# Up projections of a two-level fast product: where the first half's weight sums stand, which bank the last product uses, and who makes two of those sums

## The chip, the cores and the metric

The kernel runs on one core of one Trainium2 chip. The metric is device time in microseconds (us) of one launch. TensorE multiplies, VectorE (DVE in the rows) adds and subtracts, ScalarE (ACT) copies and applies activations, GpSimd (POOL) issues the accumulating transfers and copies small edges, SyncE (SP) issues the plain loads.

## The reference, cut to what matters

One inference step of a two-layer decoder trunk in float32, for 512 prompt rows and 32 sample rows. Each layer has a token mixer and a convolutional feed-forward part, and this is the part that the change touches:

```
u = h @ w_up                      # 544 x 1024 times 1024 x 8192
c = conv_b + sum(conv_w[j] * full[:, j:j + T] for j in range(3))
y = gelu(c[..., :4096]) * c[..., 4096:]
out = y @ w_down
```

## The kernel before

The up projection of a layer is cut into 32 groups g. A group is 128 columns of the gelu side ("a") and 128 of the gate side ("g"), over all 544 tokens, and is computed as a 2 x 2 block product with seven block products in place of eight (the Winograd form of Strassen's scheme): sums of weight blocks and sums of token blocks are multiplied, and DVE joins the products afterwards. Tokens are split in halves of 272.

From group 4 on, two groups make a "set" s (`DEEP`, 14 sets in a layer, groups 2s and 2s+1). In a set, product 1 and product 2 of both groups are themselves split: for z = 0 (gate-side weights) and z = 1 (sums of the a side), seven small products of 136 tokens (`deep_products`, in the order 1, 2, 6, 7, 5, 3, 4) take their weights from blocks of the ring and from four weight sums s3, s1, s2, s4 in `DS[z]`, and their tokens from `HT` and from four token sums in `DT`. DVE makes the weight sums (`deep_sums(s, z)`) one set ahead, ACT copies the first small product (`deep_copy`), and DVE joins the seven (`deep_joins`).

Then `deep_group` runs the remaining five products of each group, in the order 4, 1, 3, 5, 6, each into one PSUM bank (`deep_bank`). Product 6 shares the bank of product 1, so TensorE holds it until DVE has read product 1:

```
return 4 * (g % 2) + {4: 2, 1: 1, 3: 0, 5: 3, 6: 1}[j]
...
pe.wait_ge(s_ev, EV0[l] + 7 * u + 2)
product(deep_bank(g, 6), s4, b22, True, True).then_inc(s_pr, 1)
```

`s_ev` counts DVE's seven joins of a group in the order u2 (reads product 4), three of u3 (the first reads product 1), c11 (product 3), c21 (product 5), c12 (product 6).

Weights come in 1 MB loads into a ring of four slots, two slots a set. SP issues both loads of set s+1 when set s-1's products have ended, so at the start of set s: first the a side, then the g side. POOL issues two kinds of accumulating transfers: `first_sums`, which adds one half of the a-side slot to the other (512 KB, semaphore `s_sig1`; z = 1's sums of set s+1 and later weight sums wait for it), and `third_sums`, which adds a block of `w_up` to a base that SP has loaded (256 KB each, `s_base3` and `s_sig3`). POOL's queue also holds the small copies of the convolution's edges.

DVE's order in a set is written by hand in its `deep(s)`:

```
deep_part(s, g0, ("u2",))
deep_sums(s + 1, 0)
deep_part(s, g0, ("u3", "c11", "c21", "c12"))
deep_sums(s + 1, 1)
deep_part(s, g1, ("u2",))
deep_weights(g0 + 2, ("s2", "s4"))
```

and it goes on with the convolution and gate of group 2s, u3 and c11 of group 2s+1, another weight sum, and c21 of 2s+1; c12 of 2s+1 is the first work of the next set. `deep_sums(s + 1, 0)` waits for the g-side load, `deep_sums(s + 1, 1)` for `s_sig1`. ACT's order in a set begins with the convolution's first tap of group 2s-1, a side (`newest`, waits for that group's c21), then the copy of z = 0's first small product; TensorE's small product 3 of z = 0, which goes into the same bank as the copied one, waits for that copy.

Of the kernel before, what the change touches and what calls it, by code (L numbers as in the profile page):

```python
# [14 lines left out]
ALU = mybir.AluOpType  # L15
# [225 lines left out]
def trunk(nc, A, O, at, n_const):  # L241
    ctx = ExitStack()
    with ctx:
# [305 lines left out]
        s_cst2, s_tkm, s_md1, s_sne, s_sna, s_cp, s_cpe, s_qx, s_tkv, s_row = s_kce, s_kc, s_t1, s_gl, s_t2, s_bp, s_bpe, s_at, s_ate, s_imp  # L549
        s_lp, s_ls, s_lc, s_lt, s_xl = (sem(n) for n in ("s_lp", "s_ls", "s_lc", "s_lt", "s_xl"))  # L550
        s_base3 = s_wbk
        s_sig1, s_sig3 = ([sem(f"{n}{b}") for b in range(2)] for n in ("s_sig1", "s_sig3"))
        s_sop, s_soe, s_soo = (sem(n) for n in ("s_sop", "s_soe", "s_soo"))
        s_fp, s_fo = sem("s_fp"), sem("s_fo")
# [2044 lines left out]

        def deep_bank(g, j):  # L2600

            return 4 * (g % 2) + {4: 2, 1: 1, 3: 0, 5: 3, 6: 1}[j]

        def deep_copied(l, s, z):

# [34 lines left out]
        def _(sp):  # L2640
# [54 lines left out]
            def ffn_loads(l):  # L2695

                sp.wait_ge(s_mm, (M_AO0 + 3, M_MO0 + 1)[l])
                if l == 0:
                    sp.wait_ge(s_kvo, 16 * (1 + 2 * NB))
                rows = A["state_ffn_conv"][l].rearrange("b r (t c q) -> c (b r) t q", c=8, q=P)  # L2700
                for c in range(8):
                    sp.dma_start(SI[16 * c:16 * c + 16], rows[c]).then_inc(s_sil, 16)

                def third_bases(g0):
                    for g in (g0, g0 + 1):
                        c = sum_columns(g) + FF
                        sp.wait_ge(s_pr, deep_done(l, g - 2, 1))
                        sp.dma_start(WS[g % 2][:, 1], w_up[l][:, 0:4, c:c + P]).then_inc(s_base3[g % 2], 16)

                for k in range(32):  # L2710
                    k0 = W_UP[l] + k
                    i, j = divmod(k, 4)
                    if i == 0:
                        sp.wait_ge(s_mm, (M_AO, M_MO)[l] + 2 * (j + 1))
                    else:
                        sp.wait_ge(s_pr, PR0[l] + 7 * (FU * l + 4 * (i - 1) + (2, 2, 4, 4)[j]))
                    col = i * 512 + (j // 2) * 256 + (j % 2) * FF
                    sp.dma_start(R[:, k0 % RING], w_up[l][:, :, col:col + 256]).then_inc(s_w[k0 % RING], 16)
                    if i and j % 2:
                        third_bases(2 * (k // 2))  # L2720
                    if l == 0 and k == 3:
                        sp.wait_ge(s_nrm, normed(1, 1) + 8)
                        sp.dma_start(hsc[:, :], XTF[:, :]).then_inc(s_xl, 16)
                for d in range(FD):
                    if d < 3:
                        sp.wait_ge(s_pr, PR0[l] + 7 * (FU * l + (30, 30, 32)[d]))
                    else:
                        sp.wait_ge(s_mm, M_DN[l] + d - 2)
                    sp.dma_start(R[:, DN_RING[d % 3]], w_dn[l][d % 4, :, :, (d // 4) * 256:(d // 4 + 1) * 256])\
                        .then_inc(s_dw[d % 3], 16)  # L2730
                    if l == 0 and d == 4:
                        sp.wait_ge(s_xl, 16)
                        sp.dma_start(XTF[:, :], hsc[:, :]).then_inc(s_xl, 16)
# [18 lines left out]
        def _(pe):  # L2752
# [336 lines left out]
            def ffn(l):  # L3089
# [62 lines left out]
                def deep_group(s, g):  # L3152

                    u, z, e = FU * l + g, g % 2, deep_set(l, s, g % 2)
                    a11, a12, a21, a22 = up_blocks(l, g)
                    s2, s3, s4 = (WS[g % 2][:, q] for q in range(3))
                    su = SU0[l] + 4 * (u + FD * l)
                    pe.wait_ge(s_su, su + 3)
                    pe.wait_ge(s_lc, 4 * e + 3)
                    product(deep_bank(g, 4), s2, t2, True, True).then_inc(s_pr, 1 if z else 5)  # L3160
                    pe.wait_ge(s_sig3[g % 2], third_sum(l, g))
                    product(deep_bank(g, 1), s3, t3, True, True).then_inc(s_pr, 1)
                    product(deep_bank(g, 3), a12, b21, True, True).then_inc(s_pr, 1)
                    pe.wait_ge(s_lc, 4 * e + 4)
                    product(deep_bank(g, 5), a22, t4, True, True).then_inc(s_pr, 1)
                    pe.wait_ge(s_su, su + 4)
                    pe.wait_ge(s_ev, EV0[l] + 7 * u + 2)
                    product(deep_bank(g, 6), s4, b22, True, True).then_inc(s_pr, 1)

                def deep(s):  # L3170
# [6 lines left out]
                        pe.wait_ge(s_ev, EV0[l] + 7 * u)  # L3177
                    else:
                        pe.wait_ge(s_ev, EV0[l] + 7 * (u - 1))
                    pe.wait_ge(s_lt, 4 * (l + 1))  # L3180
                    deep_products(s, 0)
                    pe.wait_ge(s_sig1[s % 2], first_sum(l, 2 * s))
                    pe.wait_ge(s_ev, EV0[l] + 7 * u)
# [56 lines left out]
                def bank_free(cp, j):  # L3240
                    u = FU * (l + 1)
                    if cp == 0:
                        pe.wait_ge(s_ev, EV0[l] + 7 * (u - 2) + (5, 7, 1, 6, 12, 14, 8)[j])
                    elif cp == 1 and j == 0:
                        pe.wait_ge(s_ev, EV0[l] + 7 * u)
                    else:
                        c, q = divmod(7 * cp + j - 8, 7)
                        c += 4 * l
                        if q in (0, 3, 4):
                            pe.wait_ge(s_da, 3 * c + (1, 0, 0, 2, 3)[q])  # L3250
                        else:
                            pe.wait_ge(s_de, 7 * c + (0, 1, 6, 0, 0, 2, 7)[q])
# [422 lines left out]
        def _(dve):  # L3675
# [444 lines left out]
            def ffn(l):  # L4120
# [68 lines left out]
                def deep_tokens():  # L4189
# [4 lines left out]
                        dve.wait_ge(s_xl, 16)  # L4194
                    dve.wait_ge(s_xs, XB0[l] + 5 * l + 2)
                    x = HT[:, 0:4, :].rearrange("p k (z q t) -> p k z q t", z=2, q=2)
                    x11, x12, x21, x22 = (x[:, k:k + 2, :, q, :] for k in (0, 2) for q in range(2))
                    t1, t2, t3, t4 = (DT[:, n] for n in range(4))
                    tt(t1, x12, x11, sub).then_inc(s_lt, 1)
                    tt(t3, x22, x12, sub).then_inc(s_lt, 1)  # L4200
                    dve.wait_ge(s_lt, 4 * l + 1)
                    tt(t2, x22, t1, sub).then_inc(s_lt, 1)
                    dve.wait_ge(s_lt, 4 * l + 3)
                    tt(t4, x21, t2, sub).then_inc(s_lt, 1)

                def deep_sums(s, z):
# [9 lines left out]
                        dve.wait_ge(s_sig1[s % 2], first_sum(l, 2 * s))  # L4216
                    if e >= 2:
                        dve.wait_ge(s_lp, 7 * (e - 2) + 7)
                    tt(s3, w11, w21, sub).then_inc(s_ls, 1)
                    tt(s1, w21, w22, add).then_inc(s_ls, 1)  # L4220
                    dve.wait_ge(s_ls, 4 * e + 2)
                    tt(s2, s1, w11, sub).then_inc(s_ls, 1)
                    dve.wait_ge(s_ls, 4 * e + 3)
                    tt(s4, w12, s2, sub).then_inc(s_ls, 1)

                def deep_weights(g, names):

# [23 lines left out]
                def deep_joins(s, z):  # L4251
# [13 lines left out]
                    tt(both.rearrange("p (a b t) -> p a b t", a=2, b=2)[:, :, 1, :], pair(DU[z]),  # L4265
                       PS[:, 4 * z:4 * z + 3:2, 0:q], add).then_inc(s_lc, 1)
                    dve.wait_ge(s_lp, 7 * e + 7)
                    tt(both[:, 2 * q:3 * q], DU[z][:, q:2 * q], PS[:, 4 * z + 3, 0:q], add).then_inc(s_lc, 1)

                def deep_part(s, g, names):  # L4270

# [2 lines left out]
                    p1, q7, q5 = P1T[g % 2], Q7T[g % 2], Q5T[g % 2]  # L4274
                    ua, ug = U[:, 2 * (g % 2), :], U[:, 2 * (g % 2) + 1, :]
                    ps = lambda j: PS[:, deep_bank(g, j), 0:HALF]
                    for name in names:
                        if name == "c11":
                            dve.wait_ge(s_pr, deep_done(l, g, 3))
                            dve.wait_ge(s_ul, 2 * (u - 1))  # L4280
                            tt(ug[:, 2:2 + HALF], p1, ps(3), add).then_inc(s_ev, 1)
                        elif name == "u2":
                            dve.wait_ge(s_lc, 4 * deep_set(l, s, 1) + 4)
                            dve.wait_ge(s_pr, deep_done(l, g, 4))
                            tt(DU[g % 2], p1, ps(4), sub).then_inc(s_ev, 1)
                        elif name == "u3":
                            dve.wait_ge(s_ev, ev + 1)
                            dve.wait_ge(s_pr, deep_done(l, g, 1))
                            tt(q7, DU[g % 2], ps(1), add).then_inc(s_ev, 1)  # L4289
                            tt(DU[g % 2], DU[g % 2], q5, sub).then_inc(s_ev, 1)  # L4290
                            dve.wait_ge(s_ev, ev + 2)
                            second_half(ua, q5, q7, sub).then_inc(s_ev, 1)
                        elif name == "c21":
# [2 lines left out]
                        else:  # L4296
                            dve.wait_ge(s_ev, ev + 3)
                            dve.wait_ge(s_pr, deep_done(l, g, 6))
                            second_half(ug, DU[g % 2], ps(6)).then_inc(s_ev, 1)

                def deep(s):

# [8 lines left out]
                    convolved(g0 - 1)  # L4311
                    deep_joins(s, 1)
                    gated(g0 - 1)
                    deep_part(s, g0, ("u2",))
                    deep_sums(s + 1, 0)
                    deep_part(s, g0, ("u3", "c11", "c21", "c12"))
                    deep_sums(s + 1, 1)
                    deep_part(s, g1, ("u2",))
                    deep_weights(g0 + 2, ("s2", "s4"))
# [138 lines left out]
        def _(pool):  # L4458
# [41 lines left out]
            def ffn(l):  # L4500
# [10 lines left out]
                def first_sums(g):  # L4511
# [2 lines left out]
                    pool.dma_start(R[:, ka % RING, 0:4, :], R[:, ka % RING, 4:8, :], accum_op=ALU.add)\  # L4514
                        .then_inc(s_sig1[g // 2 % 2], 16)

                def third_sums(g):
                    pool.wait_ge(s_base3[g % 2], 64 + third_sum(l, g))
                    c = sum_columns(g)
# [3 lines left out]
                for g in range(FU):  # L4523
                    k = FU * l + g
                    if g + 1 in BY_DMA:
                        third_sums(g + 1)
                    if g + 2 in BY_DMA and g % 2 == 0:
                        first_sums(g + 2)
                    for ag in range(2):
                        n = g + 32 * ag  # L4530
# [52 lines left out]
```

## Time and profile before

| what | us |
|---|---|
| median of 3 runs (lowest, highest) | 2100.52 (2100.24, 2101.18) |
| the profiled execution's own time | 2101.75 |
| span of its trace | 2100.0 |
| TensorE busy | 2051.7 (98%) |
| VectorE busy | 1429.6 (68%) |

The trace covers the span, and the profiled execution's own time is 1.75 us more. Sums below are made against that execution, which is 1.2 us above the median of the runs.

### The profile page before, as it was taken

To read this page: it belongs to the slowest core of one execution; us is meant where nothing else is said; L and a number is where in the kernel's file an instruction comes from. 1 tells how busy PE (TensorE), PEld (TensorE's weight loads), DVE (VectorE), ACT (ScalarE), POOL (GpSimd) and SP (SyncE) were. 2 spreads that over 40 slices of the span, in tenths; PEclk is the share of its full clock that TensorE was granted. 3 is DMA by queue.
4 is the path that set the end of the run, shared out by engine and by line. 5 is a ranking of instruction groups with operands and counts; after the bars stand their busy time and mean duration, and the time that the engine had idled before them with its cause. 6 is when DMAs were issued, how large, how long until landed. Compare 5 with 4: busy or idle time off the path is not lost.

```text
span 2100.0 us, 32975 instructions
## 1 busy us (share of the span) xinstructions
PE 2051.7 (98%) x11958; PEld 1647.9 (78%) x11958; DVE 1429.6 (68%) x3462; ACT 590.0 (28%) x1362; POOL 273.6 (13%) x583
## 2 busy tenths in 40 slices
PE   8999999998899999999999999999999999999998
PEld 7556777787788888888888775778888888888887
DVE  5257996677887888888323684655888888885223
ACT  3016886563321211221001220542311222210002
POOL 1002000000022222220000100410222222210001
PEclk9999999999999999999999999999999999999999
DMA  9128206994356666662321324253366666632223
GB/s 222 56 65 261 65 2 156 277 252 93 123 126 141 141 141 149 142 141 88 130 89 63 134 81 102 71 157 92 108 141 141 143 149 158 155 95 81 81 81 117
DMA packets 270962, 262.81 MB, mean 125 GB/s; under 512 B 42802, under 2 KB 251930, under 8 KB 270034
## 3 DMA queue, kind: packets, MB, share of 16 engines
q1 hardware_dynamic: 233186, 213.58, 35.3%
q0 software_dynamic: 37616, 47.12, 11.8%
q8 instruction: 97, 1.59, 0.3%
q14 instruction: 63, 0.52, 0.1%
HBM read 230.14 MB, written 24.16 MB: 121 GB/s over the span
## 4 chain that ended last, share of the span: by engine, by line
PE 88%; DVE 4%; DMA 3%; ACT 1%; SPq 1%; issue 1%; DVEq 0%; ACTq 0%
PE PS L3107 47%; PE PS L3149 7%; PE PS L1889 3%; PE PS L863 2%; PE PS L2906 2%; PE PS L1681 2%; PE PS L2885 2%; DMA ring<-in_w_ffn_up 2%; PE PS L1760 2%; PE PS L791 2%; PE PS L778 2%; PE PS L811 2%; PE PS L1633 2%; PE PS L3046 1%; PE PS L2915 1%
## 5 line engine op out<-in xcount | busy, mean ns | idle before, releaser
L3107 PE MATMUL PS<-arena,ring 128*128 128x272 f32 x1392 | 341.6, 392 | 0.0
L3107 PEld LDWEIGHTS PS<-arena,ring 128*128 128x128 f32 x1392 | 264.3, 190 | 54.5
L3570 ACT ACTIVATE arena<-arena,CB,CW 128x560 f32<-128x560 f32 x128 | 108.5, 853 | 392.2 <-DVE arena L4295 326.1
L4172 DVE SCALAR_TENSOR_TENSOR arena<-arena,CW 128x560 f32<-128x560 f32 x256 | 187.9, 796 | 0.8 <-ACT arena L3570 0.8
L3107 PE MATMUL PS<-arena,CONST 128*128 128x272 f32 x768 | 187.1, 392 | 0.0
L3107 PE MATMUL PS<-arena 128*128 128x272 f32 x768 | 186.8, 392 | 0.0
L3107 PEld LDWEIGHTS PS<-arena,CONST 128*128 128x128 f32 x768 | 145.9, 190 | 30.1
L3107 PEld LDWEIGHTS PS<-arena 128*128 128x128 f32 x768 | 143.8, 190 | 27.8
L3107 PE MATMUL PS<-HT,ring 128*128 128x272 f32 x640 | 158.9, 393 | 2.3 <-DVE HT L4097 2.3
L3107 PEld LDWEIGHTS PS<-HT,ring 128*128 128x128 f32 x640 | 121.2, 190 | 28.1 <-ACT arena L3502 1.8
L4539 POOL COPY arena<-arena 128x16 f32<-128x16 f32 x128 | 42.1, 329 | 506.9 <-DVE arena L4295 404.2
L3107 PE MATMUL PS<-HT,arena 128*128 128x272 f32 x384 | 96.5, 394 | 4.1 <-DVE RR L4289 2.9
L3107 PE MATMUL PS<-HT,CONST 128*128 128x272 f32 x384 | 97.9, 398 | 2.1 <-DVE RR L4289 2.1
L3575 ACT ACTIVATE arena<-arena 128x560 f32<-128x560 f32 x64 | 43.0, 672 | 180.1 <-DVE arena L4172 180.1
L3107 PEld LDWEIGHTS PS<-HT,arena 128*128 128x128 f32 x384 | 71.9, 190 | 22.1 <-issue 7.8
L3107 PEld LDWEIGHTS PS<-HT,CONST 128*128 128x128 f32 x384 | 70.6, 190 | 23.4 <-issue 10.5
L3149 PE MATMUL PS<-XT 128*128 128x136 f32 x672 | 87.0, 279 | 0.0
L4082 DVE TENSOR_TENSOR arena<-ring 128x512 f32<-128x512 f32 x18 | 12.4, 690 | 109.0 <-PE PS L3107 109.0
L3149 PEld LDWEIGHTS PS<-XT 128*128 128x128 f32 x672 | 82.0, 190 | 0.0
L3636 ACT COPY RT<-PS 128x272 f32<-128x272 f32 x15 | 5.8, 386 | 270.8 <-PE PS L3107 270.8
L1121 ACT ACTIVATE arena<-arena 128x128 f32<-128x128 f32 (+3 forms) x128 | 70.7, 560 | 4.6 <-DVE arena L1275 4.6
L863 PE MATMUL PS<-arena 128*128 128x256 f32 x256 | 67.0, 386 | 2.1 <-DVE arena L1344 1.8
(609 smaller groups left out, 3827.5 us busy)
## 6 DMA issues: line engine op xcount, KB each, us to landing
ring<-in_w_ffn_up SPq DMA_DIRECT2D x64, 1024.0 KB, 6.4
ring<-in_w_ffn_down SPq DMA_DIRECT2D x32, 1024.0 KB, 5.2
ring<-in_cache_nsa_kv SPq DMA_DIRECT2D x128, 128.0 KB, 5.5
arena<-in_cache_nsa_kv SPq DMA_DIRECT2D x56, 256.0 KB, 6.7
ring<-ring POOLq DMA_DIRECT2D x28, 512.0 KB, 7.4
ring<-in_w_ml_in SPq DMA_DIRECT2D x12, 1024.0 KB, 6.8
arena<-in_cache_nsa_win SPq DMA_DIRECT2D x16, 512.0 KB, 6.7
out_nsa_win_sample<-in_cache_nsa_win POOLq DMA_DIRECT2D x8, 1016.0 KB, 17.9
```

What stands on the lines that cost most here:

```text
L778: last = mm(PS[:, 2 * (p % 2) + g2, c0:c0 + w], QT[rows, n, i * P:(i + 1) * P], KTS[rows, br - 1, n // 4, 0:w], start=True, stop=True)
L791: last = tr(PS[:, 4 + g2, k * P:(k + 1) * P], PB[:, u % 6, k * P:(k + 1) * P], ident)
L811: last = mm(out(g2, i), KVP[:, k, c0:c0 + 64], PTS[:, (2 * p + g2) % 4, s0 + k * P:s0 + (k + 1) * P], start=(p % NU == 0 and m == 0), stop ...
L863: last = mm(PS[:, 2 + c, 0:256], W1[:, c, a_, :], CT[:, (16 * n + 8 * b + a_) % 3, :, c, :], start=(a_ == 0), stop=(a_ == 7))
L1121: last = nc.scalar.activation(PB[:, u % 6, cols], SB[:, u % 4, cols], ACT.Exp, scale=-1.0, bias=ST[:, p % 4, 0, m, g2:g2 + 1], accum_out=S ...
L1889: last = mm(PS[:, bank, 0:HALF], R[:, r, k, (m % 2) * P:(m % 2 + 1) * P], turned_heads(k)[:, half(h)], start=(k == 0), stop=(k == KT - 1))
L3107: last = mm(PS[:, bank, 0:HALF], lhs[:, k, :], rhs(k), start=(first and k == 0), stop=(done and k == 3))
L3149: last = mm(PS[:, 4 * z + bank, half_], lhs[:, k, :], rhs[:, k, :], start=(k == 0), stop=(k == 1))
L3570: nc.scalar.activation(CV[:, 2 * (g % 2) + ag, :], U[:, 2 * (g % 2) + ag, 2:562], ACT.Identity, bias=cb[:, l, n:n + 1], scale=cw[:, l, 2, ...
L3575: nc.scalar.activation(CV[:, 2 * (g % 2), :], CV[:, 2 * (g % 2), :], ACT.Gelu_apprx_tanh)\
L4172: v.scalar_tensor_tensor(out=c, in0=U[:, 2 * (g % 2) + ag, tap:tap + 560], scalar=cw[:, l, tap, n:n + 1], in1=c, op0=ALU.mult, op1=ALU.add)\
L4539: g_.tensor_copy(ULS[:, n, :].rearrange("p (b r) -> p b r", b=NB), u[:, 514:562].rearrange("p (b s) -> p b s", b=NB)[:, :, 4:6])
```

## The change

- `deep_bank` puts product 6 into product 4's bank, and TensorE's wait ahead of product 6 is for one join of its group (u2) where it was for two. The waits of the down projection's first products for free banks (`bank_free`) are renumbered to match.
- In DVE's `deep(s)`, u3 of group 2s stands ahead of `deep_sums(s + 1, 0)`.
- For z = 0, s1 and s3 become plain sums of two blocks, w21 + w22 and w11 + w21. From set 3 on (13 sets a layer) DVE doesn't make them: SP loads two bases of 128 KB each into `DS[0]` (`deep_bases`, after the two ring loads), and POOL issues one accumulating transfer of 256 KB on top (`deep_accumulated`), ahead of `first_sums`. DVE waits for its semaphore `s_dsa` in `deep_sums(s + 1, 0)` and makes only s2 and s4.
- Signs follow: the token sums for z = 0 differ from those for z = 1, so `deep_tokens` has nine half-sized instructions for four, and some joins add where they subtracted.

```
-            return 4 * (g % 2) + {4: 2, 1: 1, 3: 0, 5: 3, 6: 1}[j]
+            return 4 * (g % 2) + {4: 2, 1: 1, 3: 0, 5: 3, 6: 2}[j]
+        def deep_got(l, s):
+            return 16 * (s - DEEP[0] + l * (len(DEEP) - 1))
...
+                def deep_bases(s):
+                    e = deep_set(l, s, 0)
+                    if e >= 2:
+                        sp.wait_ge(s_lp, 7 * (e - 2) + 7)
+                    c = sum_columns(2 * s) + FF
+                    for n in range(2):
+                        sp.dma_start(DS[0][:, n], w_up[l][:, 0:2, c + P * n:c + P * n + P]).then_inc(s_dsb, 16)
...
                     if i and j % 2:
+                        if k // 2 > DEEP[0]:
+                            deep_bases(k // 2)
                         third_bases(2 * (k // 2))
...
-                    pe.wait_ge(s_ev, EV0[l] + 7 * u + 2)
+                    pe.wait_ge(s_ev, EV0[l] + 7 * u + 1)
                     product(deep_bank(g, 6), s4, b22, True, True).then_inc(s_pr, 1)
...
-                        pe.wait_ge(s_ev, EV0[l] + 7 * (u - 2) + (5, 7, 1, 6, 12, 14, 8)[j])
+                        pe.wait_ge(s_ev, EV0[l] + 7 * (u - 2) + (5, 2, 7, 6, 12, 9, 14)[j])
...
-                    tt(s3, w11, w21, sub).then_inc(s_ls, 1)
-                    tt(s1, w21, w22, add).then_inc(s_ls, 1)
-                    dve.wait_ge(s_ls, 4 * e + 2)
-                    tt(s2, s1, w11, sub).then_inc(s_ls, 1)
+                    if z == 0 and s > DEEP[0]:
+                        dve.wait_ge(s_dsa, deep_got(l, s))
+                        dve.sem_inc(s_ls, 2)
+                    else:
+                        tt(s3, w11, w21, sub if z else add).then_inc(s_ls, 1)
+                        tt(s1, w21, w22, add).then_inc(s_ls, 1)
+                        dve.wait_ge(s_ls, 4 * e + 2)
+                    tt(s2, s1, w11, sub if z else add).then_inc(s_ls, 1)
                     dve.wait_ge(s_ls, 4 * e + 3)
-                    tt(s4, w12, s2, sub).then_inc(s_ls, 1)
+                    tt(s4, w12, s2, sub if z else add).then_inc(s_ls, 1)
...
-                    deep_part(s, g0, ("u2",))
+                    deep_part(s, g0, ("u2", "u3"))
                     deep_sums(s + 1, 0)
-                    deep_part(s, g0, ("u3", "c11", "c21", "c12"))
+                    deep_part(s, g0, ("c11", "c21", "c12"))
                     deep_sums(s + 1, 1)
...
+                def deep_accumulated(s):
+                    pool.wait_ge(s_dsb, 64 + 2 * deep_got(l, s))
+                    c = sum_columns(2 * s) + FF + P
+                    pool.dma_start(DS[0][:, 0:2].rearrange("p s k c -> p (s k) c"), w_up[l][:, 0:4, c:c + P], accum_op=ALU.add)\
+                        .then_inc(s_dsa, 16)
...
                     if g + 1 in BY_DMA:
                         third_sums(g + 1)
                     if g + 2 in BY_DMA and g % 2 == 0:
+                        if g // 2 + 1 > DEEP[0]:
+                            deep_accumulated(g // 2 + 1)
                         first_sums(g + 2)
```

## Rows read from the trace of the kernel before

**Rows 1.** The page, busy time of each engine, its share, instructions.

```profile
PE 2051.7 (98%) x11958; PEld 1647.9 (78%) x11958; DVE 1429.6 (68%) x3462; ACT 590.0 (28%) x1362; POOL 273.6 (13%) x583
```

**Rows 2.** TensorE's waits by releaser: total us, times, longest.

```profile
PE PS L3107 <- DVE RR L4289: 5.0, 6, 1.3
```

**Rows 3.** Busy time of one set, 869.15 to 894.10 us; PEclk, DMA share, GB/s last.

```profile
869.15:894.10 24.95, 24.95 (x138) 21.61 (x137) 20.98 (x51) 5.09 (x8) 6.41 (x15) 1.00 0.63 148
```

**Rows 4.** Timeline of TensorE in that set and the next one's start.

```profile
880.94 2.00 PE L3107 MATMUL PS<-arena,ring 128*128 128x272 f32 x8
882.78 2.00 PE L3107 MATMUL PS<-HT,arena 128*128 128x272 f32 x8
...
890.11 2.00 PE L3107 MATMUL PS<-arena,ring 128*128 128x272 f32 x8
892.00 2.07 PE L3107 MATMUL PS<-HT,CONST 128*128 128x272 f32 x8
...
896.22 0.63 PE L3149 MATMUL PS<-HT,XT 128*128 128x136 f32 x4
```

**Rows 5.** Timeline of SyncE's queue, the same stretch: issue time, length, line.

```profile
869.15 0.99 SPq L2718 DMA_DIRECT2D ring<-in_w_ffn_up  x2
...
894.10 0.99 SPq L2718 DMA_DIRECT2D ring<-in_w_ffn_up  x2
```

**Rows 6.** Timeline of DVE in the same set.

```profile
880.23 0.42 DVE L4219 TENSOR_TENSOR XT<-ring 128x256 f32<-128x256 f32 x1 [2.13 <-DMA ring<-in_w_ffn_up]
...
885.30 0.42 DVE L4219 TENSOR_TENSOR XT<-ring 128x256 f32<-128x256 f32 x1
...
886.90 0.42 DVE L4285 TENSOR_TENSOR arena<-RT,PS 128x272 f32<-128x272 f32 x1
...
894.19 0.44 DVE L4295 TENSOR_TENSOR arena<-PS,RR 128x272 f32<-128x272 f32 x1
```

**Rows 7.** Timeline of ACT at the next set's start.

```profile
894.67 0.86 ACT L3570 ACTIVATE arena<-arena,CB,CW 128x560 f32<-128x560 f32 x1 [3.17 <-DVE arena L4295]
895.43 0.25 ACT L3583 COPY arena<-PS 128x136 f32<-128x136 f32 x1
```

**Rows 8.** Timeline of POOL in the set: its two transfers before 876 us.

```profile
870.82 1.26 POOL L4520 DMA_DIRECT2D CONST<-in_w_ffn_up  x1
875.55 0.88 POOL L4514 DMA_DIRECT2D ring<-ring  x1 [3.48 <-DMA ring<-in_w_ffn_up]
```

**Rows 9.** Transfers issued from 869.1 to 869.4 us: KB, us to landing.

```profile
ring<-in_w_ffn_up SPq DMA_DIRECT2D x1, 1024.0 KB, 6.1
```

**Rows 10.** Transfers of POOL issued from 869 to 876 us.

```profile
ring<-ring POOLq DMA_DIRECT2D x1, 512.0 KB, 7.7
CONST<-in_w_ffn_up POOLq DMA_DIRECT2D x1, 256.0 KB, 9.5
```

**Rows 11.** Transfer of POOL issued from 885 to 890 us.

```profile
arena<-in_w_ffn_up POOLq DMA_DIRECT2D x1, 256.0 KB, 4.5
```

**Rows 12.** SyncE's queue in an early set, 590 to 600 us.

```profile
590.10 1.00 SPq L2718 DMA_DIRECT2D ring<-in_w_ffn_up  x2
593.77 0.37 SPq L2708 DMA_DIRECT2D arena<-in_w_ffn_up  x1
```

**Rows 13.** The landing of the transfer issued at 593.77 us.

```profile
arena<-in_w_ffn_up SPq DMA_DIRECT2D x1, 256.0 KB, 6.3
```

**Rows 14.** Timeline of DVE from 572 to 622 us.

```profile
586.92 0.72 DVE L4199 TENSOR_TENSOR XT<-HT 128x544 f32<-128x544 f32 x1
...
599.25 0.43 DVE L4219 TENSOR_TENSOR XT<-ring 128x256 f32<-128x256 f32 x1 [0.67 <-DMA ring<-in_w_ffn_up]
```

**Rows 15.** DVE from 855 to 858.5 us, a set with a late load.

```profile
855.57 0.43 DVE L4219 TENSOR_TENSOR XT<-ring 128x256 f32<-128x256 f32 x1 [3.37 <-DMA ring<-in_w_ffn_up]
```

**Rows 16.** TensorE from 391.5 to 395.3 us, outside the up projections.

```profile
394.68 0.99 PE L851 MATMUL PS<-CONST,arena 128*128 128x128 f32 x6 [2.64 <-DMA arena<-in_cache_nsa_kv]
```

**Rows 17.** Busy time from 395.4 to 398.6 us; PEclk is third from the end.

```profile
395.40:398.60 3.20, 3.20 (x19) 0.90 (x20) 1.68 (x4) 3.12 (x6) 0.00 (x0) 0.50 1.07 338
```

More of the change, by code:

```diff
@@ L551, in trunk @@
         s_base3 = s_wbk
+        s_dsb, s_dsa = s_wbv[0], sem("s_dsa")
         s_sig1, s_sig3 = ([sem(f"{n}{b}") for b in range(2)] for n in ("s_sig1", "s_sig3"))
@@ L3179, in deep @@
                         pe.wait_ge(s_ev, EV0[l] + 7 * (u - 1))
-                    pe.wait_ge(s_lt, 4 * (l + 1))
+                    pe.wait_ge(s_lt, 8 * (l + 1))
                     deep_products(s, 0)
@@ L4196, in deep_tokens @@
                     x = HT[:, 0:4, :].rearrange("p k (z q t) -> p k z q t", z=2, q=2)
-                    x11, x12, x21, x22 = (x[:, k:k + 2, :, q, :] for k in (0, 2) for q in range(2))
-                    t1, t2, t3, t4 = (DT[:, n] for n in range(4))
+                    x11, x12, x21, x22 = (x[:, k:k + 2, 0, q, :] for k in (0, 2) for q in range(2))
+                    t1, t2, t3, t4 = (DT[:, n, :, 0, :] for n in range(4))
+                    tt(t1, x11, x12, sub)
+                    tt(t3, x22, x12, sub)
+                    tt(t2, x12, x11, sub).then_inc(s_lt, 1)
+                    dve.wait_ge(s_lt, 8 * l + 1)
+                    tt(t2, t2, x22, sub).then_inc(s_lt, 1)
+                    dve.wait_ge(s_lt, 8 * l + 2)
+                    tt(t4, x21, t2, add).then_inc(s_lt, 2)
+                    x11, x12, x21, x22 = (x[:, k:k + 2, 1, q, :] for k in (0, 2) for q in range(2))
+                    t1, t2, t3, t4 = (DT[:, n, :, 1, :] for n in range(4))
                     tt(t1, x12, x11, sub).then_inc(s_lt, 1)
                     tt(t3, x22, x12, sub).then_inc(s_lt, 1)
-                    dve.wait_ge(s_lt, 4 * l + 1)
+                    dve.wait_ge(s_lt, 8 * l + 5)
                     tt(t2, x22, t1, sub).then_inc(s_lt, 1)
-                    dve.wait_ge(s_lt, 4 * l + 3)
+                    dve.wait_ge(s_lt, 8 * l + 7)
                     tt(t4, x21, t2, sub).then_inc(s_lt, 1)
@@ L4267, in deep_joins @@
                     dve.wait_ge(s_lp, 7 * e + 7)
-                    tt(both[:, 2 * q:3 * q], DU[z][:, q:2 * q], PS[:, 4 * z + 3, 0:q], add).then_inc(s_lc, 1)
+                    tt(both[:, 2 * q:3 * q], DU[z][:, q:2 * q], PS[:, 4 * z + 3, 0:q], add if z else sub).then_inc(s_lc, 1)
                 def deep_part(s, g, names):
@@ L4276, in deep_part @@
                     ps = lambda j: PS[:, deep_bank(g, j), 0:HALF]
+                    minus = g % 2 == 1
                     for name in names:
@@ L4280, in deep_part @@
                             dve.wait_ge(s_ul, 2 * (u - 1))
-                            tt(ug[:, 2:2 + HALF], p1, ps(3), add).then_inc(s_ev, 1)
+                            if minus:
+                                tt(ug[:, 2:2 + HALF], ps(3), p1, sub).then_inc(s_ev, 1)
+                            else:
+                                tt(ug[:, 2:2 + HALF], p1, ps(3), add).then_inc(s_ev, 1)
                         elif name == "u2":
@@ L4284, in deep_part @@
                             dve.wait_ge(s_pr, deep_done(l, g, 4))
-                            tt(DU[g % 2], p1, ps(4), sub).then_inc(s_ev, 1)
+                            tt(DU[g % 2], p1, ps(4), add if minus else sub).then_inc(s_ev, 1)
                         elif name == "u3":
@@ L4288, in deep_part @@
                             dve.wait_ge(s_pr, deep_done(l, g, 1))
-                            tt(q7, DU[g % 2], ps(1), add).then_inc(s_ev, 1)
-                            tt(DU[g % 2], DU[g % 2], q5, sub).then_inc(s_ev, 1)
+                            if minus:
+                                tt(q7, ps(1), DU[g % 2], sub).then_inc(s_ev, 1)
+                            else:
+                                tt(q7, DU[g % 2], ps(1), add).then_inc(s_ev, 1)
+                            tt(DU[g % 2], DU[g % 2], q5, add if minus else sub).then_inc(s_ev, 1)
                             dve.wait_ge(s_ev, ev + 2)
@@ L4298, in deep_part @@
                             dve.wait_ge(s_pr, deep_done(l, g, 6))
-                            second_half(ug, DU[g % 2], ps(6)).then_inc(s_ev, 1)
+                            if minus:
+                                second_half(ug, ps(6), DU[g % 2], sub).then_inc(s_ev, 1)
+                            else:
+                                second_half(ug, DU[g % 2], ps(6)).then_inc(s_ev, 1)
                 def deep(s):
```

## Prediction

> **What bounds the kernel now.** Read the page first: TensorE is busy for 98% of the span and DVE for 68% [rows 1]. Then one set of the up projections by itself: TensorE 24.95 of 24.95 us, at the granted clock 1.00, which is 2.4 GHz, and DVE 20.98 [rows 3]. So TensorE sets the pace there, and DVE has 4 us of slack in each set, which an average over the span hides. Then TensorE's waits by releaser: the only ones inside the sets that return are for L4289, the first join of u3: 5.0 us in 6 waits over both layers [rows 2]. They stand ahead of product 6 of a set's first group, in the sets whose g-side weights land late, since `deep_sums(s + 1, 0)`, which needs those weights, stands ahead of u3 in DVE's order. Last, the timelines of one set on every engine and queue, with times taken from A, the issue of the set's ring loads at 869.15; the next set issues its own at A+24.95 [rows 5].
>
> **What the removed wait gives.** With product 6 in product 4's bank TensorE waits only for u2, which doesn't depend on the new weights once it stands ahead of them. The six waits go: 5.0 [rows 2]. A smaller loss goes with them in the second group: its product 6 starts 1.89 us after product 5 and takes 2.07, where the first group's takes 1.84 and 2.00 [rows 4]; that is 0.12 in each of 28 sets, 3.4. Together 8.4 us. Bounds: 5.0, if the small loss has another cause, and 10, if waits too short to be listed go as well.
>
> **What costs nothing, and why.** Signs change no instruction's size. Nine half-sized token sums for four: the four are 0.72 each [rows 14]; a 272-column sum takes 0.42 [rows 6] and follows the last by about 0.4, so 3.6 against 2.8, +0.8 a layer. DVE sits idle for 0.67 before the first g-side wait a few microseconds later [rows 14] and most of it goes there; uncovered it is 1.6 in all. DVE loses two instructions of 0.42 a set, off the path. SP's two base loads are two issues of some 0.4 behind the ring loads (0.99 for two, [rows 5]), and what they wait for, z = 0's products of the set under way, ends long before the ring loads have landed. The new 512 KB a set add 20 GB/s to 148 with the transfer engines 63% busy [rows 3].
>
> **What the new transfers cost.** Here the chain is longer than the one it replaces. Before, DVE needed the g-side load alone: it waits until 880.23, A+11.1 [rows 6]. After, it needs bases, then an accumulating transfer.
> 1. The bases are behind that load in SP's queue. An early set shows such a base of 256 KB, issued at 593.77 and landed 6.3 later, at 600.1 [rows 12, 13], 0.85 after the g-side load that DVE saw at 599.25 [rows 14]. So A+11.95.
> 2. POOL wakes and issues: the a-side load landed at A+6.1 [rows 9] and the transfer that waited for it was issued at 875.55, A+6.4 [rows 8], so 0.3. A+12.25.
> 3. The accumulating transfer of 256 KB: 4.5 with little beside it [rows 11], 9.5 under the ring loads [rows 10]. By then those have landed, so 4.5: A+16.75.
> 4. POOL can't issue `first_sums` before, though its data are there at A+6.1. It lands behind the accumulating transfer. In the trace it comes 2.9 after the one ahead of it (875.55 + 7.7 against 870.82 + 9.5, [rows 8, 10]); a base load shares those microseconds, which here is out of the way sooner, so I take 2.6, an estimate. A+19.35, where it used to be A+14.1.
>
> On DVE, `deep_sums(s + 1, 0)` after A+16.75 is two sums, 0.8 (the four take 1.6, 885.30 to 886.90, [rows 6]), then the joins c11, c21 and c12 at some 0.4 each, so A+18.75; `deep_sums(s + 1, 1)` then waits for `first_sums`. It starts at A+19.35 where the trace has 885.30, A+16.15 [rows 6]: 3.2 late.
>
> **Who waits for that.** Behind it, up to c21 of the second group (894.19, which ends at 894.63), DVE has no idle time worth a row in the trace: 9.3 us of work in a fixed order [rows 6]. So c21 is 3.2 late too. ACT's first tap waits for it (894.67), and behind that, in ACT's order, is the copy of z = 0's first small product, which ends at 895.68 [rows 7]. TensorE's small product 3 of z = 0 needs that copy and starts at 896.22 [rows 4]. The slack is 0.54, less some 0.05 for the semaphore: 0.5. So TensorE stands still for 3.2 - 0.5 = 2.7 us in its small products. c12 is the next join after c21, some 0.4 later, and releases z = 1's products, which come after small products 3 and 4: no further stall.
>
> It isn't 2.7 in every set. A is set by the end of the set before; a stall comes after A and lengthens the set, so the next set's demand is later by as much while the transfers still count from A. The stalls of two neighbouring sets therefore add up to 2.7, as 2.7 and 0 or anything between; 13 sets a layer and two layers are 13 pairs: 35 us. Bounds of the pair: 0.8, if the g-side load lands at A+9.2, as in the early set (599.25 against 590.10, [rows 12, 14]); 3.9, if it is 1.2 later than here, as in the set where DVE waits 3.37 for it and not 2.13 [rows 6, 15]. In whole: 10 to 51 us.
>
> Sum: 2101.75 - 8.4 + 35 = 2128.3 for the profiled execution; the median is 1.2 below it, so 2127 for the median, 1.26% above 2100.5.
>
> A page of the Trainium skill speaks for a shorter chain (DMA: Bandwidth & Descriptors, section Anatomy of one DMA): about 2 us fixed plus the bytes at 436 GB/s for a transfer issued by GpSimd, so an estimate of 2.6 us for 256 KB and 3.2 for 512 KB. The trace has 4.5 and 7.7 [rows 10, 11] and doesn't agree; by the page `first_sums` would land near A+16.8 and the sum would be near 2095.
>
> **Rivals.**
> *The sums land in time; faster.* If the accumulating transfer takes 3 us and `first_sums` lands by A+16.6, no stall is left, only the 8.4: 2092. For it: both would run when the ring loads are done, as no row shows the two together. Against: 4.5 is already the row of a quiet stretch [rows 11], and steps 1 and 2 alone use 12.25 of the 16.6. It decides at 16.6.
>
> *Gain and cost cancel; no change.* With a pair's stall near 0.65 the cost is 8.4: 2100. It needs `first_sums` at A+17.3, two microseconds under my sum; the g-side load at A+9.2 would bring that, but only the early set, with no third sum beside its ring loads, shows it [rows 12, 14].
>
> *The stalls feed on themselves; slower still.* A wait of 2.64 us of TensorE elsewhere [rows 16] is followed by a stretch of 3.2 us at the granted clock 0.50, 1.2 GHz [rows 17]. If stalls of 2.7 do that in one set of each pair, each costs half of such a stretch more, 1.6 x 13 = 21: 2148. If, besides, the stalls don't halve because something in the chain counts from TensorE's later products, it is 2.7 x 26 = 70: 2162. Against: the stalls can settle at 1.35 each, about the longest wait of [rows 2]. The Trainium skill (TensorE: Matmul & The Clock Gate, section HAM oscillation — how this bites in real kernels) says that repeated idle gaps put the clock down again each time; the one row here agrees in kind.
>
> *The change doesn't do what it says*: the waits for u3 could turn into waits for u2, which is delayed by the first set's joins; but u2 is done before the g-side wait begins, over 4 us before product 6 starts [rows 4, 6]. It would leave out the gain: 2135, inside my range.
>
> **How the numbers follow.** About 0.2%, 4 us, is what a measurement of this kernel can tell from no change. Stalls that add up to some 2.7 a pair, or less or more within the bounds: 0.65, with its own range 2102 to 2146. Worse, by the clock or unhalved: 0.12. Cancelled: 0.08. In time: 0.15. So slower 0.77, same 0.08, faster 0.15. The range reaches from 2095, which takes in the cancelled case, to 2149; it leaves out most of the faster case and the end of the worse one, about 0.2.
>
> **What would show it.** Right: no wait for L4289 ahead of product 6; in the sets from the second on DVE idle for some 4 us ahead of the two sums s2 and s4 and again ahead of `deep_sums(s + 1, 1)`; `first_sums` issued near A+13.5 and landed past A+18; TensorE idle ahead of small product 3 of z = 0, released by ACT's copy; neighbouring sets of about 26.3 us on average. Wrong: bases that land well before the g-side load, so that SP's queue isn't served in order; an accumulating transfer of 3 us; sets of 24.9 us throughout; or a granted clock under 1.00 in the sets.

## The result: 2.45% slower, and the profile after

The changed kernel takes 2153.12 us (median of 6 runs), the kernel before, in the same sessions, 2100.38; the ratio is 1.0245, 95% interval 1.0222 to 1.0268, which is a cost of 51 us. One of the six runs, 2382.67 us at a granted clock of 0.849, was slow and stands outside the ratio, and the median of the other five is 2150.23. The forecast was 2127 in a range of 2095 to 2149; the time lies 4 us past the upper end, or 1 us by the five.

Read first where TensorE waits in the profile after (line, releaser, total us, times, longest):

```profile
PE PS L3164 <- ACT arena L3598: 41.8, 18, 4.0
```

That is small product 3 of z = 0, held by ACT's copy, 18 times where the trace before had none. The waits for u3's first join, which [rows 2] showed, are gone. Two neighbouring sets, by busy time (columns as in [rows 3]):

```profile
724.00:748.82 24.82, 24.82 (x138) 21.69 (x137) 17.08 (x41) 4.32 (x7) 7.11 (x16) 1.00 0.76 170
748.82:778.33 29.51, 26.73 (x138) 23.43 (x137) 23.76 (x58) 5.76 (x9) 7.71 (x16) 0.94 0.65 143
```

The first takes 24.82 us, 0.13 less than before [rows 3]: the small loss in the second group's product 6 is gone. The second takes 29.51, and its mean granted clock is 0.94. So one set of a pair gains a little and the other loses 4.6. Now the transfers. SP's queue in both sets, then POOL's in the first, with A = 724.00, from their timelines:

```profile
724.00 0.99 SPq L2731 DMA_DIRECT2D ring<-in_w_ffn_up  x2
727.24 0.91 SPq L2721 DMA_DIRECT2D XT<-in_w_ffn_up  x2
...
748.82 0.99 SPq L2731 DMA_DIRECT2D ring<-in_w_ffn_up  x2
755.90 0.96 SPq L2721 DMA_DIRECT2D XT<-in_w_ffn_up  x2
```

```profile
736.17 1.28 POOL L4558 DMA_DIRECT2D XT<-in_w_ffn_up  x1 [9.12 <-DMA XT<-in_w_ffn_up]
736.92 1.43 POOL L4552 DMA_DIRECT2D ring<-ring  x1
```

and the landing times of those two (KB, us from issue):

```profile
XT<-in_w_ffn_up POOLq DMA_DIRECT2D x1, 256.0 KB, 4.7
ring<-ring POOLq DMA_DIRECT2D x1, 512.0 KB, 6.4
```

In the first set the bases are issued at A+3.2; in the second, where TensorE stands in z = 0's products, 7.1 us after its ring loads, as SP waits for these products first. POOL stands 9.12 us for the bases. It issues at A+12.2, the sums land at 740.9, A+16.9, and `first_sums` lands at 743.3, A+19.3. DVE, ACT and TensorE follow in their timelines:

```profile
741.10 0.42 DVE L4250 TENSOR_TENSOR XT<-XT,ring 128x256 f32<-128x256 f32 x1 [5.66 <-DMA XT<-in_w_ffn_up]
...
743.36 0.42 DVE L4247 TENSOR_TENSOR XT<-ring 128x256 f32<-128x256 f32 x1 [0.27 <-DMA ring<-ring]
...
752.26 0.43 DVE L4330 TENSOR_TENSOR arena<-PS,RR 128x272 f32<-128x272 f32 x1
```

```profile
752.73 0.85 ACT L3585 ACTIVATE arena<-arena,CB,CW 128x560 f32<-128x560 f32 x1 [3.17 <-DVE arena L4330]
753.49 0.25 ACT L3598 COPY arena<-PS 128x136 f32<-128x136 f32 x1
```

```profile
749.55 1.55 PE L3164 MATMUL PS<-XT 128*128 128x136 f32 x12
753.88 1.08 PE L3164 MATMUL PS<-HT,XT 128*128 128x136 f32 x4 [2.78 <-ACT arena L3598]
```

DVE waits 5.66 us for the sums that POOL makes, works through s2, s4 and three joins, waits again for 0.27 us for `first_sums`, and starts z = 1's sums at A+19.36 (before: A+16.15, [rows 6]). c21 ends at 752.69, ACT's tap and copy follow, and TensorE stood for 2.78 us. That DVE is held by the accumulated sums far more than by `first_sums` goes for the whole layer; its waits for the two from 616 to 970 us:

```profile
DVE XT L4250 <- DMA XT<-in_w_ffn_up: 44.6, 10, 6.1
DVE XT L4247 <- DMA ring<-ring: 3.3, 8, 1.4
```

Then the clock, just after the wait and over the stretch that follows (PEclk third from the end):

```profile
754.10:757.40 3.30, 3.30 (x16) 3.30 (x16) 2.48 (x6) 0.67 (x2) 0.98 (x1) 0.50 1.17 315
757.50:808.60 51.10, 47.93 (x257) 41.46 (x256) 37.80 (x91) 8.88 (x14) 13.35 (x30) 1.00 0.67 145
```

0.50 is 1.2 GHz. The matmuls behind the wait run at half speed, which adds about 1.7 us to the 2.78. Over the whole span the mean granted clock fell too, here after and before:

```profile
core 0: 2154.2 us, clock 0.989
core 0: 2100.0 us, clock 0.997
```

A loss of 0.011 of 2154 us against 0.003 of 2100 is some 17 us more (an estimate, as the clock has three digits).

### The profile page after: what moved, and what is told of

It is laid out like the page before. It is cut to its first block and busy times, and to the rows that moved or that the text cites. A ratio compares the mean times of both kernels' runs of the same rounds, so it can differ in the third digit from the quotient of the medians.

```text
span 2154.2 us, 33039 instructions
## 1 busy us (share of the span) xinstructions
PE 2068.4 (96%) x11958; PEld 1670.2 (78%) x11958; DVE 1414.5 (66%) x3420; ACT 588.5 (27%) x1362; POOL 298.6 (14%) x609
## 5 line engine op out<-in xcount | busy, mean ns | idle before, releaser
L4250 DVE TENSOR_TENSOR XT<-XT,ring 128x256 f32<-128x256 f32 x56 | 23.9, 426 | 96.6 <-DMA XT<-in_w_ffn_up 95.5
L3164 PE MATMUL PS<-HT,XT 128*128 128x136 f32 x224 | 40.5, 308 | 41.8 <-ACT arena L3598 41.8
```

The costliest lines, as they stand in the source:

```text
L3164: last = mm(PS[:, 4 * z + bank, half_], lhs[:, k, :], rhs[:, k, :], start=(k == 0), stop=(k == 1))
L4250: tt(s2, s1, w11, sub if z else add).then_inc(s_ls, 1)
```

## The experiments

Letters as in the forecast: A is the issue of a set's ring loads. Each ratio is against the kernel before on the same chip (median 2098.72 us for the first four runs below, 2099.45 for the last three), with its 95% interval. What a run saves or costs is worked out from the ratios, since the chips differ.

**The accumulated sums back to DVE** (bank, order and signs stay).

```
-                        if k // 2 > DEEP[0]:
-                            deep_bases(k // 2)
...
-                        if g // 2 + 1 > DEEP[0]:
-                            deep_accumulated(g // 2 + 1)
...
-                    if z == 0 and s > DEEP[0]:
-                        dve.wait_ge(s_dsa, deep_got(l, s))
-                        dve.sem_inc(s_ls, 2)
-                    else:
-                        tt(s3, w11, w21, sub if z else add).then_inc(s_ls, 1)
...
+                    tt(s3, w11, w21, sub if z else add).then_inc(s_ls, 1)
...
```

> The changed kernel with the two accumulated sums given back to DVE (no bases, no accumulating transfer; bank, order and signs stay). Theory (the transfers' chain makes first_sums and so DVE's c21 late, and TensorE waits in small product 3): no stall is left and the product 6 waits are gone too, 2092 us (2089 to 2096), every set about 24.8 us. Rival (the order of u3, the bank or the nine token sums cost the time): stays above 2130 us.

2091.73 us, ratio 0.9959 (0.9945 to 0.9973): 0.41% or 8.6 us faster than before. TensorE over twelve sets:

```profile
650.00:950.00 300.00, 300.00 (x1645) 262.10 (x1644) 255.25 (x606) 61.48 (x97) 77.82 (x182) 1.00 0.64 150
```

It has no gap left. So the whole loss, and more, comes with the transfers; the bank, the order, the signs and the nine token sums cost nothing that shows.

**The bank alone**, on the kernel before.

```
-            return 4 * (g % 2) + {4: 2, 1: 1, 3: 0, 5: 3, 6: 1}[j]
+            return 4 * (g % 2) + {4: 2, 1: 1, 3: 0, 5: 3, 6: 2}[j]
...
-                    pe.wait_ge(s_ev, EV0[l] + 7 * u + 2)
+                    pe.wait_ge(s_ev, EV0[l] + 7 * u + 1)
...
-                        pe.wait_ge(s_ev, EV0[l] + 7 * (u - 2) + (5, 7, 1, 6, 12, 14, 8)[j])
+                        pe.wait_ge(s_ev, EV0[l] + 7 * (u - 2) + (5, 2, 7, 6, 12, 9, 14)[j])
```

> The kernel before with product 6 in product 4's bank, TensorE's wait for u2 alone and the renumbered bank_free; nothing else. Theory (u2 already stood ahead of the weight sums, so the bank alone removes the waits): 2092 us (2089 to 2096), no wait ahead of product 6. Rival (u3 has to move ahead of the weight sums as well): 2098 to 2101 us.

2092.03 us, ratio 0.9966 (0.9954 to 0.9978), 7.1 us faster; its interval overlaps that of the run above. The new bank gives the gain by itself, and u3's new place adds nothing that the measurement can tell.

**`first_sums` ahead of the new transfer** in POOL's queue.

```
+                        first_sums(g + 2)
                         if g // 2 + 1 > DEEP[0]:
                             deep_accumulated(g // 2 + 1)
-                        first_sums(g + 2)
```

> The changed kernel with first_sums ahead of the new accumulating transfer in POOL's queue. Theory A (both transfers are late, first_sums by 3.2 us and the two weight sums' path by 2.6): first_sums lands near A+13.5 again, the accumulating transfer near A+16.9 still, a pair of sets loses about 2 us and not 3 to 5, and few stalls are long enough for the clock to fall: 2115 to 2130 us. Rival B (only the late first_sums costs): 2092 us. Rival C (the added traffic costs, whatever its order): 2150 us.

2174.89 us, ratio 1.0345 (1.0322 to 1.0368). None of the three: slower than the changed kernel. SP's and POOL's queues in a set with A = 810.49, and the landing of the second base (issued at about 814.2):

```profile
813.73 0.96 SPq L2721 DMA_DIRECT2D XT<-in_w_ffn_up  x2
```

```profile
816.75 0.88 POOL L4552 DMA_DIRECT2D ring<-ring  x1 [3.21 <-DMA ring<-in_w_ffn_up]
825.71 1.28 POOL L4558 DMA_DIRECT2D XT<-in_w_ffn_up  x1 [8.08 <-DMA XT<-in_w_ffn_up]
```

```profile
XT<-in_w_ffn_up SPq DMA_DIRECT2D x1, 128.0 KB, 11.2
```

`first_sums` is now issued at A+6.3, and beside its 512 KB the second base lands at 825.4, A+14.9, where POOL had it by A+12.2 in the changed kernel. The new transfer goes out at A+15.2, 3 us later than there. I had taken its landing as unmoved, and that was wrong: what one transfer wins, the bases lose. It is so beyond this set: of the eight sets of this run with bases issued at A+3.2, seven have the new transfer's issue at A+13.6 to 15.8; in the changed kernel's eight it is at A+11.8 to 13.6. DVE's wait for it and TensorE's waits in that run:

```profile
830.41 0.43 DVE L4250 TENSOR_TENSOR XT<-XT,ring 128x256 f32<-128x256 f32 x1 [8.48 <-DMA XT<-in_w_ffn_up]
```

```profile
PE PS L3164 <- ACT arena L3598: 51.4, 17, 4.0
PE PS L3122 <- DVE arena L4317: 9.4, 9, 1.6
```

The second line is new: u2 of the second group, queued on DVE behind the late sums, now holds product 6. Accumulated sums this late are enough for a loss; a late `first_sums` isn't needed for one.

**The bases between the two ring loads** (same transfers, same bytes).

```
                     col = ...
+                    if i and j % 2 and k // 2 > DEEP[0]:
+                        deep_bases(k // 2)
                     sp.dma_start(R[:, k0 % RING], ...)
                     if i and j % 2:
-                        if k // 2 > DEEP[0]:
-                            deep_bases(k // 2)
                         third_bases(2 * (k // 2))
```

> The changed kernel with SP issuing the two bases between the a-side and the g-side ring load (same transfers, same bytes). Theory (what costs is that the bases stand behind the g-side load): bases land near A+7.5, the accumulating transfer near A+13 to 14, first_sums near A+16, which DVE can bear (A+16.6): 2092 to 2102 us. Rival C (the added traffic costs): 2145 us or more.

2102.79 us, ratio 1.0018 (1.0009 to 1.0028), just past the upper end of what the theory expected. SP's and POOL's queues in a set with A = 844.34, and the landings of POOL's two and of the g-side load:

```profile
844.34 0.37 SPq L2733 DMA_DIRECT2D ring<-in_w_ffn_up  x1
847.63 0.91 SPq L2721 DMA_DIRECT2D XT<-in_w_ffn_up  x2
848.58 0.53 SPq L2733 DMA_DIRECT2D ring<-in_w_ffn_up  x1
```

```profile
852.61 1.27 POOL L4558 DMA_DIRECT2D XT<-in_w_ffn_up  x1 [5.17 <-DMA XT<-in_w_ffn_up]
```

```profile
ring<-ring POOLq DMA_DIRECT2D x1, 512.0 KB, 7.3
XT<-in_w_ffn_up POOLq DMA_DIRECT2D x1, 256.0 KB, 5.3
ring<-in_w_ffn_up SPq DMA_DIRECT2D x1, 1024.0 KB, 8.1
```

The new transfer goes out at A+8.3 and lands at A+13.6. The g-side load is put off in turn: it is issued at A+4.2, behind the bases and what they wait for, and lands at A+12.3, still ahead of the sums. The edit takes 48 of the changed kernel's 51 us off, with every byte still moved: the place in the queue costs, not the traffic. What is left is the same wait, shorter:

```profile
PE PS L3164 <- ACT arena L3598: 8.8, 11, 2.1
```

**The copy first**, in ACT's order of the changed kernel.

```
+                    deep_copy(s, 0)
                     newest(g0 - 1, (0,))
-                    deep_copy(s, 0)
                     newest(g0 - 1, (1,))
```

> The changed kernel with ACT's copy of z = 0's first small product ahead of the convolution's first tap in ACT's order; nothing else. Theory (TensorE stands in small product 3 because that copy is queued behind a tap that waits for DVE's late c21): the wait for the copy goes, and the next that is late is z = 1's wait for c12, with about 1.5 us more slack: a pair loses some 1.3 us and the clock stays up: 2100 to 2112 us. Rival (DVE as a whole is behind and TensorE will wait elsewhere by as much): 2145 us or more.

2112.07 us, ratio 1.0062 (1.0045 to 1.008), at the upper end. Two lines changed places on ACT and 38 us went, though the transfers are nearly as late as before (`first_sums` lands at A+17.6 to 20.1, in the changed kernel at A+18.8 to 21.0). TensorE's longest item:

```profile
PE PS L3164 <- DVE arena L4143: 18.5, 15, 1.9
```

This is z = 1's first product, which waits for c12: the next that is late, as expected, by less than half as much.

**Bases between and copy first**, both edits.

> Bases between the two ring loads and the copy first, both. Theory: the 8.8 us of waits for the copy that the bases between leave are gone, and no other takes their place: 2091 to 2095 us, as the bank alone gives. Rival (added traffic or DVE's lateness keep a cost): 2099 to 2103.

2092.8 us, ratio 0.9966 (0.9954 to 0.9978): as fast as the bank alone, with both weight sums made by transfers. All of the change's cost is accounted for by its place in SP's queue and the order on ACT. Nothing is won by the transfers either: DVE has less to do, but isn't what bounds.

```profile
650.00:950.00 300.00, 298.96 (x1638) 261.03 (x1637) 242.02 (x576) 60.49 (x96) 90.93 (x194) 1.00 0.76 171
```

**The stalls filled with work**, for the clock's share.

```
-                        for k in range(2):
-                            last = mm(...)
+                        for _ in range(4 if j == 5 and z == 0 and s > DEEP[0] else 1):
+                            for k in range(2):
+                                last = mm(...)
```

> The changed kernel, but small product 5 of z = 0 is computed four times over, with the same result, from set 3 on: 12 more matmuls of 136 columns, 1.36 us of work for TensorE in each of 26 sets, where it would stand still in one set of two. Theory (the stalls' length is set by the transfers, and the falls of the clock that follow the long ones are a price on top): the work fills the waits, none is long enough for the clock to fall, a pair of sets still loses about 3 us: 2125 to 2140 us, faster than the changed kernel's 2153 with more work. Rival (the clock costs nothing here, because the time is set by the transfers and DVE anyway): 2150 to 2156. Rival (stalls and work simply add): 2185.

2137.71 us, ratio 1.0176 (1.0161 to 1.0192). 35 us more work for TensorE (26 times 1.36), and the time falls by some 14 against the changed kernel. A stretch of each layer, and the wait that is left (41.8 in the changed kernel):

```profile
650.00:950.00 300.00, 297.50 (x1671) 260.98 (x1670) 228.58 (x542) 55.47 (x89) 79.20 (x177) 1.00 0.71 158
1580.00:1850.00 270.00, 267.44 (x1502) 234.60 (x1501) 206.07 (x488) 50.58 (x81) 71.89 (x160) 1.00 0.72 159
```

```profile
PE PS L3165 <- ACT arena L3599: 7.7, 14, 1.3
```

The clock stays at 1.00. The added work and the waits that are left come to 43 us, about what the waits alone were; what is gone is the half clock. The same two stretches of the changed kernel:

```profile
650.00:950.00 300.00, 284.49 (x1510) 248.80 (x1510) 226.15 (x533) 56.04 (x89) 81.13 (x176) 0.97 0.70 154
1580.00:1850.00 270.00, 255.39 (x1377) 222.47 (x1376) 205.37 (x487) 50.17 (x81) 73.33 (x160) 0.99 0.71 158
```

## Why the prediction was wrong, point by point

- *What the removed wait gives, 8.4 us*: right. By the ratios it is 8.6 with the new order and 7.1 for the bank alone.
- *What costs nothing*: right in the sum, for the signs, the order and the token sums by the run without the transfers, and for the traffic by the run with both edits. One premise was wrong: the bases' wait for z = 0's products ends late in a set that stalls (7.1 us after its ring loads, above). POOL issues there 11.3 us after them, no later than elsewhere, so no cost of it shows.
- *The chain of transfers*: right in each step. Foretold and, in the set shown: POOL's issue A+12.25 and 12.2; the accumulating transfer's landing 16.75 and 16.9; `first_sums` 19.35 and 19.3; DVE's start on z = 1's sums 19.35 and 19.36. That it is as close as this is luck of the set: over the 26 sets POOL issues at A+11.1 to 13.6, the sums land at A+15.8 to 18.5 and `first_sums` at A+18.8 to 21.0. The shorter chain that the page DMA: Bandwidth & Descriptors of the Trainium skill would give, in its section Anatomy of one DMA (2.6 us for 256 KB, an estimate from its figures), is not what the trace has: 4.7.
- *Who waits*: right. Small product 3 through ACT's copy, 2.78 us where 2.7 was worked out, and the copy's place on ACT is shown by its own run. That a stall spares the next set is right too.
- *The stalls, 35 us*: mis-sized a little. They sum to 41.8, or 3.2 a pair of sets and not 2.7; the single waits go up to 4.0. The set that the term was worked from was a mild one: DVE's wait for the g-side load, 2.13 there [rows 6], is 2.4 on average in that layer of the trace before (30.8 us in 13 waits).
- *The clock, at nothing in the sum*: this is the step that failed. I left it to a rival at 0.12 with the reason that the stalls "can settle at 1.35 each". Mostly they don't. The trace after has ten half-clock stretches in the sets or at their ends, nine of 3.4 us and one of 6.8; they sum to 37.5 us, at half speed a loss of 18.8. Eight of them have a set behind them that could stall, and none of these does (29.51 and 24.82 above): the stall with the slow stretch lengthens its set by enough that the next one's demand comes after the transfers. Where a stall has no such stretch behind it (1.88, 2.51, 1.72 and 2.75 us), the next set stalls for 0.5 to 1.0. A granted clock under 1.00 in the sets was named as a sign of being wrong, and it is there. The rival priced the clock at 21 us, 1.6 in 13 sets, which was near; its chance was not. That the clock costs some 14 us here is shown by the filled stalls, which pay for 35 us of added work. The Trainium skill (TensorE: Matmul & The Clock Gate, section HAM oscillation — how this bites in real kernels) says that repeated gaps put the clock down again and again; the trace agrees in ten waits of twelve.

Sum with the measured terms: 2101.75 - 8 + 41.8 + 18.8 = 2154.4, beside 2156.01 for the profiled execution. Without the clock's term it is 2135.6, inside the range; with it and the stalls as forecast it would be 2147.6, inside as well. The time left the range because both terms fell short, the clock by 18.8 and the stalls by 6.8.

The rivals that ended faster or equal needed `first_sums` by A+16.6 or A+17.3, and it lands at A+18.8 at the earliest: the bases do stand behind the g-side load, and the accumulating transfer takes 4.7 us and not 3. Moving the bases ahead of that load is what gives the time back. The rival that left out the gain is refuted by the run with the bank alone.

## What to carry to other kernels

Work that is moved from an engine with slack to a queue is priced by the queue's order: here the transfer was as late as the load in front of its bases made it, and what stood behind it in the program order of each engine that it passed (SP, POOL, DVE, ACT) became late too. Follow that chain to the first engine that can't wait, and look whether a small reorder there takes it off, as one copy ahead of one tap did here for 38 of 51 us. And when a forecast leaves TensorE standing for waits of this size in a loop, put the half-clock stretch behind them into the sum; don't leave it to a rival.

## What was not expected of the hardware

- In the changed kernel twelve waits of TensorE in the sets are of 2.2 us or longer (2.27 to 3.96), and ten of them have a stretch at the granted clock 0.50 that begins within 1 us of their end; two (2.51 and 2.75, at 1584 and 1691 us) have none. With the copy first, a wait of 1.91 us (at 951 us) has one, so the length of a wait alone doesn't tell. A set's half-clock stretch cost more than half of the wait before it (1.7 against 2.78).
- With `first_sums` first, its 512 KB went out on POOL's queue 2.5 us after SP had issued the second base, and still put the base's landing off from before A+12.2 to A+14.9. So a transfer issued later and on another queue delayed one that was under way in SP's.
